# Forgetting attention on one Trainium2 core: the widest probability tile of each head goes from GpSimd to VectorE, and the copies of its transposes from VectorE to ScalarE

## The reference

```python
log_f = jax.nn.log_sigmoid(f_logit + f_bias)
c = jnp.cumsum(log_f, axis=1)            # per head, along the tokens
s = (q * HEAD_DIM ** -0.5) @ k.T + c[query] - c[key]
p = softmax(where(key <= query, s, -inf))
o = p @ v                                # per head
```

## Time and profile before

| | |
|---|---|
| median of 3 runs | 2368.73 us (2367.63 to 2368.8) |
| the profiled execution | 2362.22 us, its span 2360.5 us |
| PE busy | 2119.1 us (90%) |
| DVE / ACT / POOL busy | 1167.5 / 731.9 / 440.5 us |
| the forgetting attention | from 1042 us to 1133 us of the span |
| mean granted TensorE clock | 0.925 of full speed |

### The profile page before, as it was taken

The page is one execution under the profiler, slowest core; times in us unless marked ns, Lnnn a source line. Parts: engine busy times, 40 slices in busy tenths (PEclk is TensorE's granted clock), DMA queues, the critical chain, the costliest instruction groups (busy, mean ns, idle before and its releaser), DMA issues.

```text
span 2360.5 us, 25614 instructions
## 1 busy us (share of the span) xinstructions
PE 2119.1 (90%) x9416; PEld 1626.8 (69%) x9416; DVE 1167.5 (49%) x2097; ACT 731.9 (31%) x1228; POOL 440.5 (19%) x338
## 2 busy tenths in 40 slices
PE   8977999789999978998889999959999687999996
PEld 6766667668788766875678887845445536888875
DVE  4332345576346343237566256262406654867744
ACT  3210345323223213245243123122213205443441
POOL 2100000000000000039100000000020004767774
PEclk9985789789999998999989999979999897999998
DMA  5231100135335312210235235211110002233333
GB/s 203 90 116 45 27 19 19 54 127 184 116 106 197 107 54 107 96 49 2 108 126 194 89 134 203 109 56 37 72 71 36 18 36 90 107 121 111 125 127 122
DMA packets 39828, 224.91 MB, mean 95 GB/s; under 512 B 5920, under 2 KB 6368, under 8 KB 20144
## 3 DMA queue, kind: packets, MB, share of 16 engines
q1 hardware_dynamic: 27840, 181.17, 21.3%
q0 software_dynamic: 11888, 42.39, 5.7%
HBM read 215.61 MB, written 2.10 MB: 92 GB/s over the span
## 4 chain that ended last, share of the span: by engine, by line
PE 80%; DVE 10%; POOL 5%; ACT 3%; issue 1%; DMA 1%; SPq 0%; POOLq 0%; DVEq 0%; ACTq 0%
PE G L401 33%; PE G L1934 7%; PE TR L1934 4%; PE OB L1934 4%; PE G L905 3%; PE G L1857 3%; PE G L1661 3%; PE OB L1682 2%; POOL SC_sb L682 2%; PE G L1876 2%; PE OB L1004 1%; PE G L1832 1%; DVE stat_sb L2381 1%; PE G L1995 1%; PE G L907 1%
## 5 line engine op out<-in xcount | busy, mean ns | idle before, releaser
L401 PE MATMUL G<-xt_high,weights_high 128*128 128x512 f32 x1128 | 450.0, 399 | 21.1 <-DVE weights_low L424 16.1
L401 PE MATMUL G<-xt_low,weights_high 128*128 128x512 f32 x1128 | 444.0, 394 | 0.0
L401 PE MATMUL G<-xt_high,weights_low 128*128 128x512 f32 x1128 | 443.5, 393 | 0.0
L424 DVE TENSOR_TENSOR weights_low<-ring_sb,weights_high 128x1024 fp32r<-128x1024 f32 x196 | 234.9, 1206 | 385.4 <-ACT weights_high L418 385.3
L418 ACT ACTIVATE weights_high<-ring_sb 128x1024 fp32r<-128x1024 f32 x284 | 293.8, 1044 | 373.8 <-PE OB L1934 136.9
L401 PEld LDWEIGHTS G<-xt_high,weights_high 128*128 128x128 f32 x1128 | 213.8, 190 | 71.4 <-issue 23.4
L401 PEld LDWEIGHTS G<-xt_low,weights_high 128*128 128x128 f32 x1128 | 213.8, 190 | 47.5 <-issue 3.5
L401 PEld LDWEIGHTS G<-xt_high,weights_low 128*128 128x128 f32 x1128 | 213.6, 189 | 46.7 <-issue 1.4
L424 POOL TENSOR_TENSOR weights_low<-ring_sb,weights_high 128x1024 fp32r<-128x1024 f32 x88 | 213.1, 2437 | 74.0 <-ACT weights_high L418 74.0
L1426 DVE SCALAR_TENSOR_TENSOR KS_sb<-G,cols_sb,KS_sb 128x441 f32<-128x441 f32 (+2 forms) x176 | 120.8, 686 | 75.1 <-ACT KS_sb L1182 75.1
L1599 POOL DMA_DIRECT2D KS_sb<-ada x64 | 33.8, 529 | 572.6 <-DVE og_sb L2280 572.6
(11 more groups left out here) (432 smaller groups left out, 3677.4 us busy)
## 6 DMA issues: line engine op xcount, KB each, us to landing
ring_sb<-chunks SPq DMA_DIRECT2D x142, 1024.0 KB, 4.8
KS_sb<-ada POOLq DMA_DIRECT2D x64, 512.0 KB, 4.7
ring_sb<-slabs SPq DMA_DIRECT2D x10, 2048.0 KB, 7.8
qb_sb<-wide_sb SPq DMA_DIRECT2D x24, 128.0 KB, 2.2
X_sb<-x SPq DMA_DIRECT2D x4, 512.0 KB, 6.6
rows_sb<-ln_gain POOLq DMA_DIRECT2D x4, 512.0 KB, 5.3
rows_sb<-ln_bias POOLq DMA_DIRECT2D x4, 512.0 KB, 6.0
out<-X_sb SPq DMA_DIRECT2D x4, 512.0 KB, 4.9
```

Source lines behind the costliest of these rows:

```text
L401: mm = nc.tensor.matmul(out, lhsT=a, rhs=b, start=(3 * i + j == 0), stop=(3 * i + j == n - 1))
L424: tt_(out=Wl[:, n % 4, c], in0=raw_quarter(Q)[:, c], in1=Wh[:, n % 4, c], op=ALU.subtract).then_inc(w_lo, 1)
```

## The change

GpSimd no longer scales tile 3. VectorE does it, by `tensor_scalar`, right behind its copy of turn 0 and in front of its copy of turn 1. The copies of turns 4 and 5 (tile 3 of either head) go from VectorE to ScalarE, where they stand behind the exponentials of tile 3 of the next pair. TensorE's order stays as it is; its waits are counted on four semaphores in place of two. In the diff, the first `copy` and the two calls of it that are added are ScalarE's; the added `scale` is VectorE's, and the last part is GpSimd's.

```diff
         N_FOX = 8
         TURNS = [(0, (0, 1)), (1, (0, 1)), (2, (0,)), (2, (1,)), (3, (0,)), (3, (1,))]
+        SCALED_POOL = 3
...
             def turn(n, k):
                 t, es = TURNS[k]
-                pe.wait_ge(pair_scaled, 8 * n + 2 * t + es[-1] + 1)
-                if 6 * n + k >= 2:
-                    pe.wait_ge(pair_copied, 6 * n + k - 1)
+                if t < SCALED_POOL:
+                    pe.wait_ge(pair_scaled, 2 * SCALED_POOL * n + 2 * t + es[-1] + 1)
+                else:
+                    pe.wait_ge(pair_scaled_dve, 2 * (TT - SCALED_POOL) * n + 2 * (t - SCALED_POOL) + es[-1] + 1)
+                if k >= 2:
+                    pe.wait_ge(pair_copied, 4 * n + k - 1)
+                elif n:
+                    pe.wait_ge(pair_copied_act, 2 * n + k - 1)
...
             def attended(n):
-                pe.wait_ge(pair_copied, 6 * n + 6)
+                pe.wait_ge(pair_copied, 4 * n + 4)
+                pe.wait_ge(pair_copied_act, 2 * n + 2)
...
+            def copy(n, k):
+                act.wait_ge(pair_turned, 6 * n + k + 1)
+                dst, ps = turned_pair(k)
+                nc.scalar.activation(dst, ps, ACT.Copy).then_inc(pair_copied_act, 1)
...
                 exp(n + 1, 2)
                 exp(n + 1, 3)
+                copy(n, 4)
+                copy(n, 5)
...
+            def scale(n, t):
+                dve.wait_ge(pair_rec, 4 * n + t + 1)
+                for e in range(2):
+                    p = pair_scores(n, e, t)
+                    nc.vector.tensor_scalar(p, p, rsp[:, n % 2, t, e:e + 1], None, ALU.mult).then_inc(pair_scaled_dve, 1)
...
                 copy(n, 0)
+                scale(n, 3)
                 copy(n, 1)
                 mixed_low(n - 1)
                 least(n + 1, 2)
...
                 least(n + 1, 3)
                 invert(n + 1, 1)
-                copy(n, 4)
-                copy(n, 5)
...
             for n in range(N_FOX):
                 scale(n, 2)
-                scale(n, 3)
                 stage_low(n + 2)
                 scale(n + 1, 0)
                 scale(n + 1, 1)
```

More of the change, by code:

```diff
@@ L362, in build @@
         pair_turned = sem("pair_probabilities_transposed")
-        pair_copied = sem("pair_transposes_copied")
+        pair_scaled_dve = sem("pair_probabilities_scaled_by_vector")
+        pair_copied = sem("pair_transposes_copied_by_vector")
+        pair_copied_act = sem("pair_transposes_copied_by_scalar")
         pair_out = sem("pair_attended_in_psum")
@@ L504, in mixed, with turned_pair @@
             return Hl[:, 8 + k, :], Hh[:, k, :]
+        def turned_pair(k):
+            t, es = TURNS[k]
+            ps = TR[k % 2][:, 0:len(es) * (t + 1) * P].rearrange("p (u b c) -> p u b c", u=len(es), b=t + 1)
+            return PTU[:, es[0]:es[-1] + 1, 0:t + 1, t * P:(t + 1) * P], ps
         def score_bank(n, e, t):
@@ L629, in copy @@
             def copy(n, k):
-                t, es = TURNS[k]
                 dve.wait_ge(pair_turned, 6 * n + k + 1)
-                ps = TR[k % 2][:, 0:len(es) * (t + 1) * P].rearrange("p (u b c) -> p u b c", u=len(es), b=t + 1)
-                nc.vector.tensor_copy(PTU[:, es[0]:es[-1] + 1, 0:t + 1, t * P:(t + 1) * P], ps).then_inc(pair_copied, 1)
+                dst, ps = turned_pair(k)
+                nc.vector.tensor_copy(dst, ps).then_inc(pair_copied, 1)
+            def scale(n, t):
[3 more added lines that the diff above has]
+                    nc.vector.tensor_scalar(p, p, rsp[:, n % 2, t, e:e + 1], None, ALU.mult).then_inc(pair_scaled_dve, 1)
             def mixed_low(n):
```

## The result

The changed kernel takes 2370.79 us in the median of 20 runs (2367.15 to 2375.02), the kernel before 2367.48 in 20 (2365.14 to 2371.23). The ratio is 1.0015, with a 95% interval of 1.0008 to 1.0022: slower by 0.15%, under what was set as the bound of "no change", but clear of zero. The forecast was +3.7 us or 1.0016. The profiled execution took 2369.35 us, its span 2367.7; it is one execution, and further above its counterpart of before (7.1 us) than the medians are (3.3 us).

A forecast was written before the change was run, and what follows sets the result against it. GpSimd was taken to bound the stage at 10.95 us per pair, the new loop at 9.56 + 2.10 = 11.66 us. Balance 4.3 - 0.8 + 0.2 = +3.7 us on 2368.7 gave 2372.4 us, range 2365.5 to 2376.0.

The forecast's parts named there:

- The bound of before: In the forgetting attention, GpSimd alone sets the pace at 10.95 us per pair; the change takes 3.08 us off it.
- The loop of 9.56 us: From one attended to the next, through VectorE's queue, ScalarE's exponentials and copies: 9.56 us plus the two scalings.
- The sixth step: The step from attended to attended that meets no low parts: 9.56 + 0.80 = 10.36 us.
- The price of the scalings, S = 2.10: VectorE's two tile 3 scalings add 2.10 us per step, waiting beside GpSimd's two low parts; floor 0.80.
- the upper bound of 2.4: Most the two scalings could add per step, since nothing else is queued on GpSimd there: 2.4 us.
- The ground for taking 2.10 and not 1.09: The second low part goes ahead of the second scaling, giving 2.10 us; were the scaling first, 1.09.
- GpSimd's saving is lost whole: The 8 x 3.08 = 24.6 us taken off GpSimd gain nothing in the new loop.
- Rival 1: VectorE's scalings pass with little or no wait (0.80 or 1.09 us): 2365.9 to 2367.3 us; chance 0.30.
- Rival 2: TensorE's clock falls inside the loop, 0.82 us per spell in attended and turn 0; three make 2374.9 us; chance 0.25.
- The number: Whole program: 4.3 - 0.8 + 0.2 = +3.7 us, to 2372.4 us, +0.16%.
- from the first to the last `attended`: Five steps of 11.66 us, a sixth of 10.36 and a last of 7.6: 76.3 us, against 71.98 before.
- Rival 3: The loop is not closed, ScalarE's exponentials run ahead and TensorE's work is the bound: 17.3 us go, 2351; chance 0.03.

The follow-up runs named there:

- The experiment that makes it true: Changed kernel with ScalarE's mixed_high put ahead of stage_high, so GpSimd's low parts begin after VectorE's scalings start: 2361.91 us, 0.9985 of the kernel before.

## Why the prediction was right, point by point

- **The bound of before.** Right. With all scalings on GpSimd, the copies on ScalarE change nothing (1.0000), and GpSimd's queue sets the pace with its 1.54, 1.54 and 2.47. With tile 3 off GpSimd and the scalings out of the loop, a step falls from 10.95 to 9.68 us.
- **The loop of 9.56 us.** Right. The sixth step, without low parts, is 10.36 us, as forecast to the hundredth; that exactness is luck, since the terms were rounded. Early scalings leave 9.68 instead of 9.56, copies on VectorE take 0.70 more off instead of 0.68.
- **The price of the scalings, S = 2.10.** The term that decided the sign, and an estimate from other instructions. Measured, from the start of the first scaling to that of the copy of turn 1: 2.47, 2.24, 2.17 (1085.40 to 1087.57), 2.17 and 2.20. The first lies above the upper bound of 2.4. The steps are 11.74 to 11.81 us but for the first, 0.1 over the forecast. The swap of two instructions of ScalarE shows the cause.
- **The ground for taking 2.10 and not 1.09.** It was that VectorE, having waited, gets its turn between two GpSimd instructions. The row that the prediction read does not show this: the subtraction that the instruction at 2303.66 waited for was already under way (it ran from 2301.87 to 2305.29, the last of its row), and the next one began only at 2305.74. The rows that follow do show it:

```profile
2305.74 5.21 POOL L424 TENSOR_TENSOR weights_low<-ring_sb,weights_high 128x1024 fp32r<-128x1024 f32 x2 [0.45 <-ACT weights_high L418]
2306.60 2.09 DVE L1390 SCALAR_TENSOR_TENSOR X_sb<-X_sb,og_sb 128x512 f32<-128x512 f32 x1
```

  The first of these two subtractions takes 2.40 us and ends at 2308.14; VectorE's instruction ends at 2308.69, while the second, until 2310.95, is still to come. In the changed kernel this order of turns held in four steps of five.
- **GpSimd's saving is lost whole.** Right: its busy time fell by 22.5 us, the time rose.
- **Rival 1, scalings without a wait.** Refuted by the 1.48 us of the second scaling. The experiment that makes it true is faster than the kernel before by 4.3 us in the medians (2361.91 against 2366.20), by 3.5 by the ratio; the rival had 1.4 to 2.8.
- **Rival 2, the clock.** Partly there, and underpriced. In the profiled execution `attended` of the last step took 4.06 us, 1.7 more than at full clock, where the prediction had 0.82 from a spell that covered it only in part. The trace of before already held one that covered it:

```profile
1069.69 4.06 PE L550 MATMUL OB<-XT_sb,wide_sb 128*64 128x512 f32 x16
```

  What brings such a spell on is not shown: with the scalings early TensorE stood for the same 2.45 us in front of the same output, and `attended` then took 2.37 us at full clock.
- **The number.** The forecast of +3.7 us lies nearer to the medians' +3.3 than its own terms do to the profile. There the start is 0.8 us sooner, as forecast, and the end 0.1 later, but from the first to the last `attended` it takes 78.97 us and not 76.3: 1.0 more in the five steps with low parts, 1.7 in the last. So the stage is longer by 6.3 us in the profiles (1141.14 - 1042.35 = 98.8 against 1134.53 - 1042.01 = 92.5 before). How often such spells fall into the executions of either kernel was not measured; that the medians show so little of these 2.7 us is luck as far as the forecast goes.
- **Rival 3, no loop.** Excluded: TensorE waits for ScalarE's copies, and the steps are 11.7 us and not 8.5.

## What to carry to other kernels

When work is moved off the engine that is the bound, walk once round the waits from an output to the next and add up the other engines' queues: here the 3 us per step that GpSimd saved were met by a loop that was only 0.6 us shorter than the old step (10.37 against 10.95), even where the scalings waited for nothing. Put moved work where its new engine already stands idle ahead of a wait, not behind the thing that it waited for. And the 0.48 us of a float32 `tensor_scalar` of VectorE in SBUF are its price only while GpSimd is idle; beside GpSimd up to 2.92 were seen. Look at what GpSimd executes at that instant, since another engine's order two instructions away can shift it.

## What the runs showed of the hardware

VectorE's scaling, one tensor in and out of SBUF with a scalar per partition, waits for a low part of GpSimd that is under way: 0.48 us alone, 0.84 and 1.48 beside two low parts of 1.28 and 1.45. The Trainium skill has this in "SBUF — State Buffer", section "SBUF: two separate sides", as an exclusive hold for a whole instruction, and beside the low parts the trace agrees. It also agrees in the other direction: the second low part took 1.46 us where it starts right behind a scaling, and 1.27 where none came between:

```profile
1074.17 1.46 POOL L699 TENSOR_TENSOR staged_even<-wide_sb,staged_even 128x512 fp32r<-128x512 f32 x1
```

```profile
1062.00 1.27 POOL L699 TENSOR_TENSOR xt_low<-wide_sb,xt_low 128x512 fp32r<-128x512 f32 x1
```

The second of these rows belongs to something that I had not expected. The scaling that began at 1061.40 was waiting when the first low part ended at about 1062.04, and yet the second low part went ahead of it:

```profile
1061.40 2.15 DVE L660 TENSOR_SCALAR SC_sb<-SC_sb,rsp_sb 128x512 f32<-128x512 f32 x1
1063.48 0.48 DVE L660 TENSOR_SCALAR ring_sb<-ring_sb,rsp_sb 128x512 f32<-128x512 f32 x1
```

It ended at 1063.55, 0.27 after the second. So the one that waits does not always get its turn between two instructions of the other; the 2.92 us of the variant with the copies on VectorE are of the same kind, and stand in the same step. What decides it was not tried and stays open.

Beside GpSimd's own scalings the hold for a whole instruction isn't borne out. In the variant with early scalings and the copies on VectorE, GpSimd was at a scaling of tile 2 when both scalings of VectorE came:

```profile
1080.91 1.41 POOL L705 TENSOR_SCALAR SC_sb<-SC_sb,rsp_sb 128x384 f32<-128x384 f32 x1
```

```profile
1081.48 0.49 DVE L655 TENSOR_SCALAR SC_sb<-SC_sb,rsp_sb 128x512 f32<-128x512 f32 x1
1081.88 0.72 DVE L655 TENSOR_SCALAR ring_sb<-ring_sb,rsp_sb 128x512 f32<-128x512 f32 x1
```

The first ran in its own time in the middle of GpSimd's instruction, which took 1.41 us where 1.24 is its usual time; the second ended 0.28 us after it. With the scalings early and the copies on ScalarE, the second scaling (1080.61 to 1081.41) also ended within one of GpSimd's (1080.39 to 1081.80). GpSimd's times are the least exact of a profile, and no experiment here separates the cases. Nor was it tried whether a scaling that moves one element per cycle would pass beside GpSimd.
